# Low rank columns first in the rw projection, another order of ring loads, and the products before attention on VectorE alone

## The reference

```python
decay = exp(-DECAY_SCALE * sigmoid(w0 + tanh(wd) @ w_lora_up))      # per direction z
a     = sigmoid(a0 + ad @ a_lora_up)                                # per direction z
g     = sigmoid(gd) @ g_lora_up
kk    = k * k_k;  kk = kk * rsqrt(sum(kk*kk) + 1e-12)               # per head
k_dir = k * (1 + (a - 1) * k_a);  b_dir = kk * a
# scan in both directions: S = S*w - (S kk) b^T + v k^T,  y = S r
```

## Time and profile before

| | us |
|---|---|
| three runs | 1308.08, 1308.98, 1324.79 |
| median | 1308.98 |
| profiled execution | 1318.49 |
| its span (first to last instruction) | 1316.7 |
| PE busy | 1056.3 |
| DVE busy | 430.4 |

### The profile page before, as it was taken

How to read it: one execution, slowest core, us unless ns; L and a number is a source line. 1 busy time by engine, 2 the same in 40 slices (tenths; PEclk the granted TensorE clock), 3 DMA queues, 4 the chain that set the end, 5 groups by cost and what they waited for, 6 DMA issues and landing times. The chain is left out here.

```text
span 1316.7 us, 24546 instructions
## 1 busy us (share of the span) xinstructions
PE 1056.3 (80%) x10878; PEld 641.1 (49%) x10878; DVE 430.4 (33%) x885; ACT 265.2 (20%) x496; POOL 71.2 (5%) x95
## 2 busy tenths in 40 slices
PE   1699898969638846889895688637999999999970
PEld 0265454445525545878885344433444444444430
DVE  0402532242686634363733342250101010101006
ACT  0411211123735511212212000011111111111100
POOL 6000000050000010000000000030000000000003
PEclk9899999985769976989998788858999999999985
DMA  9803415449993000000003920138789898989816
GB/s 276 304 0 128 146 46 192 156 153 401 402 403 140 17 18 3 4 12 5 4 4 101 340 105 0 64 160 315 259 314 356 312 356 314 357 314 355 315 50 239
DMA packets 95933, 244.95 MB, mean 186 GB/s; under 512 B 6612, under 2 KB 11508, under 8 KB 95328
## 3 DMA queue, kind: packets, MB, share of 16 engines
q1 hardware_dynamic: 75632, 168.83, 36.1%
q0 software_dynamic: 16160, 58.53, 11.7%
q10 hardware_dynamic: 4048, 16.18, 3.4%
HBM read 176.51 MB, written 67.01 MB: 185 GB/s over the span
## 5 line engine op out<-in xcount | busy, mean ns | idle before, releaser
L2040 PE MATMUL ps<-arena 128*128 128x512 f32 x544 | 238.4, 595 | 1.7 <-ACT arena L2090 1.7
L2040 PEld LDWEIGHTS ps<-arena 128*128 128x128 f32 x544 | 102.4, 191 | 125.8 <-issue 125.1
L649 PE MATMUL ps<-arena 128*128 128x512 f32 (+3 forms) x448 | 126.9, 443 | 9.4 <-DMA arena<-in_w_in_dram 9.4
L2054 PE MATMUL ps<-arena 128*128 128x512 f32 x272 | 122.4, 603 | 4.1 <-ACT arena L2094 4.1
L649 PEld LDWEIGHTS ps<-arena 128*128 128x128 f32 (+1 forms) x448 | 69.0, 191 | 71.2 <-issue 56.4
L1738 PE MATMUL ps<-arena 128*128 128x512 f32 x160 | 79.7, 661 | 14.7 <-DMA arena<-in_w_out_dram 10.6
L2054 PEld LDWEIGHTS ps<-arena 128*128 128x128 f32 x272 | 51.2, 193 | 63.1 <-issue 63.1
L1738 PEld LDWEIGHTS ps<-arena 128*128 128x128 f32 x160 | 33.8, 215 | 57.1 <-issue 57.1
L538 DVE SCALAR_TENSOR_TENSOR arena<-arena 128x128 f32<-128x128 f32 (+3 forms) x56 | 30.9, 552 | 93.2 <-ACT arena L427 91.7
L2131 DVE TENSOR_TENSOR arena<-arena,ps 128x512 f32<-128x512 f32 x17 | 11.7, 689 | 135.6 <-ACT arena L2086 135.6
L2139 DVE COPY arena<-ps 128x512 f32<-128x512 f32 x17 | 11.8, 692 | 127.4 <-PE ps L2054 127.4
(11 more groups left out here) (309 smaller groups left out, 1453.5 us busy)
## 6 DMA issues: line engine op xcount, KB each, us to landing
gathered_tokens<-arena POOLq DMA_DIRECT2D x16, 2560.0 KB, 55.8
arena<-in_exp_gate_dram SPq DMA_DIRECT2D x17, 2048.0 KB, 13.2
arena<-in_exp_up_dram SPq DMA_DIRECT2D x17, 2048.0 KB, 18.1
arena<-in_exp_down_dram SPq DMA_DIRECT2D x17, 2048.0 KB, 9.9
arena<-in_w_mod_dram SPq DMA_DIRECT2D x12, 2048.0 KB, 15.4
arena<-gathered_tokens SPq DMA_DIRECT2D x18, 512.0 KB, 15.6
expert_outputs<-arena ACTq DMA_DIRECT2D x17, 512.0 KB, 8.5
arena<-in_w_in_dram SPq DMA_DIRECT2D x4, 2048.0 KB, 8.3
```

Source lines behind the costliest of these rows:

```text
L649: mm = pe.matmul(ps[0:m, b, 0:hi - lo], ring[:, slot_of(what), k, (e % 4) * P:(e % 4) * P + m], hT[:, k, lo:hi], start=(k == 0), stop=(k = ...
L2040: mm = pe.matmul(ps[:, b, :], xgT[:, k, :], w[u][:, k, :], start=(k == 0), stop=(k == KT - 1))
L2054: mm = pe.matmul(ps[:, Y0 + half, :], hidT[:, k, :], wd[u][:, k, half * 512:(half + 1) * 512], start=(k == 0), stop=(k == 3))
```

## The change

Block 1. The ring's order is now a list with a slot for each piece; a piece is loaded when the one that held its slot is used up. The low rank piece `rw` 3 comes first, and PE, ACT and DVE go through e in `E_ORDER` = 12, 13, 0 to 11. The `mod2` products are spread over single pieces. ACT takes sigmoid and tanh after the eighth piece, the squares after the eleventh and the root after the thirteenth; PE's `norms`, DVE's sum and reciprocal come here too.

Block 2. PE starts with four `decay_logits` and mixes the rest with turns, sums and norms. `key_factors` is gone from ACT; `product(n, 0)` has a `tensor_scalar` for it on DVE, with a wait for its end. SP starts the zero fill. ACT starts the stores of bonus and output.

Block 3. POOL clears `Mx`, `Of`, `states[0]`; `yacc` is not cleared, the first output of a chunk is copied instead of added. PE waits only before the scan's first step, ACT for `Mx`, DVE for three.

```diff
+        E_ORDER = [12, 13] + list(range(12))
+        MOD2_AT = {3: (0,), 5: (1,), 7: (2,), 9: (3,), 11: (4,), 12: (5,), 13: (6, 7)}
+        order1 = [(("mod", 0), 0), (("mod", 1), 1), (("mod", 2), 2), (("mod", 3), 0), (("qkv", 0), 1), (("qkv", 1), 2),
+                  (("rw", 3), 0), (("rw", 0), 1), (("mod2", 0), 2), (("mod2", 1), 0), (("rw", 1), 2), (("mod2", 2), 0),
+                  (("mod2", 3), 1), (("rw", 2), 0), (("mod2", 4), 1), (("mod2", 5), 2), (("mod2", 6), 1), (("mod2", 7), 2)]
-        MOD2_AFTER = {6: (0, 1), 9: (2, 3), 12: (4, 5), 13: (6, 7)}
+        ROW_AT = {6: (0,), 7: (1,), 9: (2,), 11: (3,), 12: (4,), 13: (5, 6, 7)}
...
+                    if n == 7:
+                        act.wait_ge(qn_ok, NTT)
+                        act.wait_ge(shift_ok, 2)
+                        act.activation(gate_in[0:GATE_LORA, :], gate_in[0:GATE_LORA, :], ACT.Sigmoid)
+                        act.activation(lw_in[0:64, :], lora_in[0:64, :], ACT.Tanh).then_inc(tanh_ok, 1)
+                    if n == 10:
+                        act.wait_ge(shift_ok, 10)
+                        act.wait_ge(tq_mm, NTT)
+                        for c4 in range(NC4):
+                            act.activation(ksq[:, c4, :], rws[:, 4 + c4, :], ACT.Square, scale=kkv[:, c4:c4 + 1]).then_inc(ksq_ok, 1)
+                    if n == 12:
+                        act.wait_ge(n_ok, 1)
+                        act.activation(rk40, rk40, ACT.Sqrt).then_inc(nstd_ok, 1)
...
-                    if J >= 2:
-                        pe.wait_ge(row_ok, J - 1)
+                    if J >= 1:
+                        pe.wait_ge(row_ok, J)
...
+                for k in range(4):
+                    decay_logits(k)
                 for c in range(5):
                     turn_values(c)
...
-                def key_factors(c4):
-                    act.wait_ge(siga_ok, 2 * c4 + 2)
-                    for z in range(2):
-                        act.activation(chm[:, z, K_, c4, :], chm[:, z, B_, c4, :], ACT.Identity, bias=ka1v[:, c4:c4 + 1],
-                                       scale=kav[:, c4:c4 + 1]).then_inc(rp_ok, 1)
...
+                    if n == 7:
+                        act.wait_ge(bo_ok, NC4)
+                        act.dma_start(bonus_d, rws[:, 8:12, :].rearrange("p a t -> p (a t)")).then_inc(st_bo, 16)
...
+                    if i in (6, 7, 11, 15):
+                        store((i - 2) // 4 if i > 6 else 0)
+                store(NLAT)
...
+                        ch(dve.tensor_scalar(K__, B__, kav[:, c4:c4 + 1], ka1v[:, c4:c4 + 1], ALU.mult, ALU.add))
...
+                pool.memset(Mx, 0.0).then_inc(zeroed, 1)
                 pool.memset(Of, 0.0).then_inc(zeroed, 1)
-                pool.memset(Mx, 0.0).then_inc(zeroed, 1)
                 pool.memset(states[0], 0.0).then_inc(zeroed, 1)
-                pool.memset(yacc, 0.0).then_inc(zeroed, 1)
-                pool.wait_ge(zeroed, 4)
+                pool.wait_ge(zeroed, 2)
...
-                pe.wait_ge(zeroed, 4)
```

More of the change, by code:

```diff
@@ L221, in build @@
         MOD1, NMOD2, NRW = 4, 8, 4
[L222 to L225, removed]
+        E_ORDER = [12, 13] + list(range(12))
[3 more added lines that the diff above has]
+                  (("mod2", 3), 1), (("rw", 2), 0), (("mod2", 4), 1), (("mod2", 5), 2), (("mod2", 6), 1), (("mod2", 7), 2)]
+        slots, turn_in_slot, held_by = {}, {}, {}
+        for what, slot in order1:
+            earlier = [w_ for w_ in slots if slots[w_] == slot]
+            slots[what], turn_in_slot[what], held_by[what] = slot, len(earlier) + 1, earlier[-1] if earlier else None
         ORDER_MOD = (2, 3, 0, 1)
@@ L543, in _ @@
                                 ch(ins)
[L544 to L560, removed]
+                    if n < NTT:
+                        turned_heads(n)
@@ new lines, in _ @@
+                    if n == NTT:
+                        dve.memset(lw_in[64:65, :], 1.0).then_inc(ones_row, 1)
+                    if n == 11:
+                        dve.wait_ge(n_mm, 1)
+                        dve.tensor_scalar(rk40, ps[:, 7, 0:P], 1e-12, None, ALU.add).then_inc(n_ok, 1)
+                    for J in ROW_AT.get(n, ()):
+                        dve.wait_ge(red_mm, J + 1)
+                        dve.wait_ge(ld_brow[J % 2], 16 * (J // 2 + 1))
+                        if J >= 2:
+                            dve.wait_ge(st_row[J % 2], 16 * (J // 2))
+                        row = mrow2[0:2, J % 2, :]
+                        ins = dve.tensor_tensor(row, ps[0:2, 6, :], brow2[0:2, J % 2, :], ALU.add)
+                        if J not in (4, 5):
+                            ins.then_inc(row_ok, 1)
+                            continue
+                        ins.then_inc(row_tmp, 1)
+                        dve.wait_ge(row_tmp, J - 3)
+                        dve.wait_ge(ld_g2, 16 * (J - 3))
+                        dve.scalar_tensor_tensor(row, row, 1.0, g2row[0:2, :], ALU.add, ALU.mult).then_inc(row_ok, 1)
@@ L562, in _ @@
+                    if n == 13:
+                        dve.wait_ge(nstd_ok, 1)
+                        dve.reciprocal(rk40, rk40).then_inc(rec_ok, 1)
             @block.tensor
@@ L651, in _ @@
                     mm.then_inc(rw_mm, 1)
[L652 to L666, removed]
+                    if 1 <= n <= NTT:
+                        turn_heads(n - 1)
+                    if n == 11:
+                        norms()
+                    for J in ROW_AT.get(n, ()) if n < NET - 1 else (5,):
+                        reduce_rows(J)
+                    for J in MOD2_AT.get(n, ()):
+                        mod2(J)
+                reduce_rows(6)
+                reduce_rows(7)
         CHM = R + 4 * T + T + PAST
@@ L1561, in _ @@
                             dve.wait_ge(y_ok[1 - z], s + z)
-                        dve.tensor_tensor(ya, ya, quarter(BG2 + z), ALU.add).then_inc(y_ok[z], 1)
+                        if chunk_at(z, s) in [chunk_at(v, w) for w in range(s + 1) for v in range(2) if (w, v) < (s, z)]:
+                            dve.tensor_tensor(ya, ya, quarter(BG2 + z), ALU.add).then_inc(y_ok[z], 1)
+                        else:
+                            dve.tensor_copy(ya, quarter(BG2 + z)).then_inc(y_ok[z], 1)
                     if pieces:
```

195 lines of the change are left out of this document (92 added, 103 removed).

## The result

The changed kernel takes 1292.47 us (median of four runs, 1290.91 to 1294.34), the kernel before 1309.22 us; the ratio is 0.985, with a 95% interval of 0.981 to 0.989. Forecast were 1291.9 us. The time agrees almost to the microsecond, the stages do not all, and the profile says why. The gain of 1.5% is clear of noise.

The account below looks back on a forecast made before the run. It took PE as the bound in the rw projection and DVE in block 2's products. Terms summed to -17.1 us: 1318.5 profiled gave 1301.4, put on the median 9.5 us lower 1291.9 us; range 1277 to 1305.

Parts of the forecast that it names:

- Ring: rw projection, block 1: all three PE waits for input weights go, -9.4 us, plus slow clock after two, -1.8 and -1.7.
- Norms and the last piece: Norms moved into block 1: PE +1.6 us, one reduction fewer ahead -1.0, ACT and DVE 0; last piece ends at 256.7.
- Tail: End of block 1: row 5 left for the end and reductions sharing one bank, each waiting for the row before, +3.1 us.
- Front: Block 2 to the last rate logits: less PE idle time, norms gone, same clock mix; 46.7 us, -6.4, ending at 318.5.
- Rival A: Block 2: the clock rises; up to 19.4 us less, total 1272.5 us, or 1282 for half the stretch; chance 0.17.
- `key_factors`: Block 2, moved from ACT to DVE: eight instructions at 0.58 us, +4.6, handover gain 2.2, net +2.4 us.
- Fill: Zero fill on SP, block 2: hidden behind the block, cost 0 us.
- Rival B: Block 2: ACT held at its bonus store while SP's queue is full; total 1334 or 1321 us; chance 0.06.
- Stores: Store issues on ACT in block 2, three of five between attention's pairs: 0 to 2 us, taken 0.7.
- Block 3: Start of block 3: PE begins at the block's start instead of after the yacc memset, -4.6 us.
- Rival C: Block 1: a piece still late or PE waiting at row reductions; total 1298 or 1305 us; chance 0.10.

Follow-up runs that it names:

- b_again: The kernel before, unchanged, profiled a second time; median 1310.51 us, ratio 1.000, profiled at 1307.59 us.
- b_third: The kernel before, unchanged, for a third profile; profiled at 1312.49 us.
- slots_in_turn: The changed kernel with its order of pieces kept but ring slots taken in turn (n mod 3); 1310.74 us, ratio 0.998 to the kernel before.
- row5_early: The changed kernel with key_factors on ACT between rate sigmoids and behind exponentials 1, 3, 5, and DVE's row 5 ahead of the last shift; 1292.64 us, ratio 0.984.
- logits_first: The changed kernel with all ten decay logits at the front of block 2, ahead of turns, sums, norms and rates; one run, profiled at 1299.71 us.
- factors_first: The changed kernel with key_factors back on ACT, ahead of all exponentials as before the change; 1292.02 us, ratio 0.982.
- fill_on_pool: The changed kernel with the zero fill started by POOL and the bonus and output stores by SP, as before; 1295.68 us, ratio 0.985.
- clear_all_first: The changed kernel with block 3 started as before: POOL also clears yacc, PE, ACT and DVE wait for all four memsets; 1301.11 us, ratio 0.988.
- clumped_again: The changed kernel with block 2's front nearly as before, turns first, then decay logits in clumps of 4, 3 and 3; second profile, front 43.1 us.

## Why the prediction was right, and where it was not

The total was right because it was built from differences that mostly came true, and because it was put on the median. Taken against b_again, a profile near the median, the differences are: rw -13.4, tail +3.2, front -7.3, handover -2.9, products +5.2, attention +1.9, scan -4.3, the rest +0.6, together -16.8 of span (forecast -17.1). That it fits to a microsecond is luck. Against b_third, as good a reference, the span is 21.7 us shorter, with -7.3 in the scan; the scan and attention differ by several us between profiles of kernels that are the same there.

1. Ring: forecast 0 of 9.4 us of waits left and 3.5 us of clock back. Right; no wait for a load in the stage, clock 1.00. slots_in_turn shows the cause for two of the three waits. One term is a little too large: 19.3 us of 65 records were compared with 17.6 us of 64.
2. Norms and the last piece: forecast to end at 256.7, it ended at 255.7; PE's first stage was 0.8 us shorter by itself, and ACT's additions were hidden.
3. Tail: forecast +3.1, measured +3.2. row5_early takes 1.3 of it away by row 5 alone. The rest is read from the timeline: both reductions wait for the row before, 1.05 and 0.86 us.
4. Front: the step "if the rest runs at the same mix of clocks, it takes 46.7 us" failed. It took 37.4, so the last rate logits came at 308.4 (forecast 318.5), the first product at 312.9 (324) and attention at 353.4 (363.7). The forecast difference, -6.4, holds against a front of 44.7 as in b_again (-7.3), not against the 53.1 of the row that it was worked from (-15.7). Against b_again its two terms are there: idle time goes from 5.0 to 0.3 us (forecast -4.8), and PE's busy time is 2.6 us less, of which 1.6 were forecast for the norms; 1.0 is left for the clock. The mistake was to take one execution's clock as the kernel's. It cost the total nothing only because that execution's excess of 9.5 us, nearly all of it in this stage, had been taken off with the median. Rival A, with 0.17, was true of the level reached, and half its price (10 us) is there against the first profile; it is not there in the medians, because the kernel before has nearly that clock too in two of its three profiles (0.77). The rule of "TensorE: Matmul & The Clock Gate" in the Trainium skill, Part 1, that sustained activity releases the clock, does not hold for these logits: 17.4 us of full work at 0.50 in logits_first. For the turns that follow the trace agrees: the clock is up before the first 80 records of them end, 4.12 us.
5. `key_factors`: DVE +5.2 where +4.6 was taken. An instruction took 610 ns, not 554, and its successor starts 0.64 us after it, where 0.58 was taken; the 0.03 in that figure had no row. Handover -2.9 to -3.0 where -2.2 was taken. The net of +2.3 is the forecast's +2.4 because both terms were too small by about as much; factors_first puts it at the same 2.3 by these two stages.
6. Fill: forecast hidden, end at 399; it ended at about 395. Rival B did not occur, ACT issued in 0.36 us.
7. Stores: 0.7 forecast, some 0.4 by fill_on_pool. Attention's length goes with the clock it draws: 97.2 us at 0.89 here, 94.8 at 0.93.
8. Block 3: -4.6 forecast. The start moved by 4.6 us (clear_all_first), the scan by -4.3 against b_again; clear_all_first was 0.3% slower than the change, as the start would make it, but the intervals overlap.

Rival C was wrong: no piece was late.

## What to carry to other kernels

With a ring of buffers, look at what the slot of a late load last held: a load that waits for the piece just in use is covered only by the work between that piece's end and its own first use, here 2 us of PE work against a load of some 8. Give it the slot that comes free one piece earlier.

Work moved off one engine should be put where the other one waits. Here eight instructions were worth 2.9 us off ACT's path and cost 5.2 on DVE's; kept on ACT, six of them where ACT waits for DVE anyway, they kept both gains and cost 0.7 us in the front.

Before a stage's length is used as a term, find out whether its clock is the same in another profile; differences within a stage are safer than its end.

## What the runs showed of the hardware

- TensorE fully busy with fp32 products of a 65-row stationary operand and 512 columns stayed at 1.2 GHz for 17.4 us (logits_first) and rose within the 64x64 products behind them.
- The clock also fell from 2.4 to 1.2 GHz with no idle time ahead: after 12.00 of 12.00 us busy in row5_early, and after 14.8 us busy, the last 3.4 of them at 2.4 GHz, in clumped_again. Which kind of work does that was not separated.
- The same program's stage of 310 records took 53.1, 44.7 and 44.6 us in three profiles, with a clock of 0.63 in the first and 0.77 in the other two: a spread of 8 us on one core with nothing else changed.
- A `tensor_scalar` of 128x640 with two per-partition scalars took 610 ns, with one 554 ns.
- SP spent 84 us in sixteen issues of the fill (2.5 MB each), while ACT's issue in the same time took 0.36 us. The same sixteen issues took POOL 13.8 us (fill_on_pool).
